# A hybrid RWKV-7 / latent-attention / mixture-of-experts layer: 128 stationary columns split in two column halves

## The chip, the cores and the metric

The kernel runs on one core of one Trainium2 chip. The metric is the device time of one launch in microseconds (us), the median of several runs. All times below are of that core. TensorE (PE in the profile) multiplies a stationary operand, loaded by LDWEIGHTS (PEld), with a moving operand that streams through the array. The array has 128 rows (the contraction, which is the partitions of both operands) and 128 columns (the stationary operand's columns, which become the output's partitions). An instruction can use a part of it: "64\*128" in a profile row is 64 rows by 128 columns. DVE is VectorE, ACT is ScalarE, POOL is GpSimd.

## The reference

The layer is computed for a prompt of 1024 tokens and a sample of 512 tokens, 1536 tokens in all, 12 tiles of 128. What bears on the change is the time mixing (a scan over tokens with a 64 x 64 state per head, 8 heads, both directions) and the router's logits:

```python
def step(state, inp):
    r_t, w_t, k_t, v_t, kk_t, a_t = inp
    sa = jnp.einsum('bhvk,bhk->bhv', state, -kk_t)
    state = (state * w_t[:, :, None, :] + sa[..., None] * (kk_t * a_t)[:, :, None, :]
             + v_t[..., None] * k_t[:, :, None, :])
    return state, jnp.einsum('bhvk,bhk->bhv', state, r_t)
...
kk = kk / jnp.maximum(jnp.sqrt(jnp.sum(kk * kk, axis=-1, keepdims=True)), 1e-12)   # per head of 64
w_log = -jax.nn.softplus(-(decay_w0[d] + jnp.tanh(wd) @ decay_up[d])) - 0.5
a = jax.nn.sigmoid(iclr_a0[d] + ad @ iclr_up[d])
...
g_prob = jax.nn.softmax((xt @ w_rg).astype(jnp.float32) + b_rg, axis=-1)   # 4 groups
e_logits = (xt @ w_re).astype(jnp.float32) + b_re                          # 32 experts
```

Around it stand adaLN modulation, an input projection of 1024 to 5120 columns, latent attention with 8 heads, a gated merge, an output projection, and a mixture of 32 experts with two experts for each token. Everything is float32.

## The kernel before

The stages run one after the other, each a block with one instruction stream for each engine, tied by semaphores: modulation and norm; input projection with the scan's operands (`project_in_and_operands`, to about 840 us); the scan (`wkv_scan`, about 840 to 1355 us); attention; the branch outputs; output projection with the router (about 1930 to 2240 us); the experts.

**Input projection and operands.** TensorE computes 40 column tiles of the projection in 20 pairs `i`. For each tile and each block of 512 tokens it runs 8 x 3 products of the split form (`split_product`, L97: L99, L100, L101). In the last 12 pairs, token tile `t = i - 8` of the scan's operands is made between those products: `gather_squares` (L551) sums the squares of k for each of 8 heads; its stationary operand `gather[:, f]` has 8 columns, and the four products (one for each 128 channels `f`, L558) accumulate in 8 partitions of `ps_8`. ACT takes the root (`root`, L631), DVE clamps and inverts (`inverse_norm`, L713), and `spread_inverse` (L561) sends the 8 values back to 128 partitions each through `spread`. `decay_and_rate` (L568) multiplies the decay and rate LoRA factors: four products each into `ps_w` and `ps_a`, contraction 64, one on the upper and one on the lower half of the rows (L580, L581), 128 stationary columns, 128 moving.

**The scan.** It works in chunks of 64 tokens, two chunks and both directions `d` for each tile `i` of 12. TensorE's order in an iteration `j` is written out by hand (L1072 to L1142). It interleaves three things: the sequential part of tile `j` (`from_state`, `from_values`, `update_state`, `update_output`, for `k` = 0 and 1); the inverse of a 64 x 64 triangular matrix for each head of tile `j + 1`, by doubling (`level_z` L986 and `level_xz` L995 for levels 1 to 4, then `half_product` L1004 and `cross_product` L1014), with transposes `turn_v`, `turn_bk` and the product `mask_v`; and `products` of tile `j + 2`. Filler products (`idle`, `dense`, `fill`) run in the first and last iterations only. The functions that the change touches:

- `products(i, d, c)` (L927, product at L939), four times an iteration: for each `f` and `g` a product with contraction 64 (row half `g`), 128 stationary columns and 128 moving columns, into PSUM tile `G`, bank `g`. After each, DVE masks `G` into `lbm` (`mask_products`, L1279) and only then the next `products` may write `G`.
- `mask_v(i, k)` (L966, product at L977), twice: 16 products with contraction 64, 128 stationary and 64 moving columns, into bank `r` of `G`. ACT copies `G` after each (`keep_mv`, L1199); the second `mask_v` waits for that. `half_product` stands between the two.
- `from_state(i, k)` (L1017, product at L1024), twice: 16 products of the same shape into `Q`, bank `g`. DVE forms `wkv_p` from it (L1314), and `from_values` needs that.

The inverse's doublings go through other engines too: after `level_z` ACT copies twice (`keep_z`, L1151, L1152) and then `level_xz` may run; after `level_xz` DVE adds and transposes (L1294, L1284) and then the next level may run.

A float32 product is carried out as two instructions, so a group of 16 products shows as x32 in the profile.

**The router.** In the output projection's stage, TensorE runs for each tile `t` two halves of the projection (24 split products each), and between them the ranks and `route` (L2559): 8 accumulating products over the model width, stationary the turned tokens `h2_t[:, k]` (128 columns), moving the router's 36 columns (L2564). DVE reads the logits (L2658) and picks groups and experts.

## Time and profile before

| what | us |
|---|---|
| median of 3 runs (lowest, highest) | 2669.66 (2669.62, 2692.78) |
| span of the profiled execution, first to last instruction | 2663.8 |
| median less that span (start and end of a launch, and the spread between executions) | 5.9 |
| TensorE busy in the span | 2463.5 |
| VectorE, ScalarE, GpSimd busy | 1564.1, 1042.1, 784.2 |

The page gives the profiled execution by its span alone; its time as a run is not shown apart from the three. In a row of the timeline the first number is the start of a group of like instructions, the second the time from there to the end of its last one; a matmul's length includes its way through the array, so consecutive groups overlap, and the distance from start to start tells how long a group holds TensorE. The last part in square brackets is idle time before the group and what ended it.

### The profile page before, as it was taken

The numbers are of one execution on the slowest core, as the hardware profiler recorded it, in microseconds if no ns is written. First come the engines' busy times: TensorE is split into PE (matmuls) and PEld (weight loads), VectorE is DVE, ScalarE is ACT, GpSimd is POOL, SyncE is SP. The second block draws the span as 40 slices with busy tenths as digits, with TensorE's granted clock in tenths as the row PEclk, the third lists the DMA queues.
The fourth block names the chain that finished last, engine by engine and source line by source line (L and its number), as shares of the span: only waits on it lengthen the run. The fifth ranks groups of instructions, "written<-read, shape, count | busy, mean of one in ns | idle before, by whom it ended". The sixth has DMA issues, their size and how long they took to land. (4 is left out here: it accounts for less than half of the span.)

```text
span 2663.8 us, 53179 instructions
## 1 busy us (share of the span) xinstructions
PE 2463.5 (92%) x22289; PEld 1932.3 (73%) x22289; DVE 1564.1 (59%) x2402; ACT 1042.1 (39%) x1855; POOL 784.2 (29%) x511
## 2 busy tenths in 40 slices
PE   5799999999997999999979889998988996999997
PEld 1488887788886999999978766666877884555554
DVE  3544458975663454554457566666886786544443
ACT  4311123343441455445445455554122221454443
POOL 0122245544442345335303300001300000444553
PEclk8899999999998999999999999999999997999998
DMA  8522224344434132332044431102755456899995
GB/s 336 204 85 79 79 97 145 128 151 147 143 136 164 55 83 71 97 94 71 19 133 111 119 91 33 31 22 104 242 166 204 160 168 237 288 360 351 357 321 113
DMA packets 196290, 399.27 MB, mean 150 GB/s; under 512 B 38698, under 2 KB 104010, under 8 KB 182994
## 3 DMA queue, kind: packets, MB, share of 16 engines
q1 hardware_dynamic: 173876, 322.58, 35.7%
q0 software_dynamic: 12960, 41.82, 5.9%
q10 hardware_dynamic: 9216, 31.46, 3.0%
q8 instruction: 178, 2.92, 0.5%
q14 instruction: 60, 0.49, 0.1%
HBM read 294.57 MB, written 106.48 MB: 151 GB/s over the span
## 5 line engine op out<-in xcount | busy, mean ns | idle before, releaser
L99 PE MATMUL ps_in<-h_t_low,w_in_high 128*128 128x512 f32 x960 | 379.4, 395 | 2.1 <-PEq L79 2.1
L100 PE MATMUL ps_in<-h_t_high,w_in_low 128*128 128x512 f32 x960 | 374.6, 390 | 0.0
L101 PE MATMUL ps_in<-h_t_high,w_in_high 128*128 128x512 f32 x960 | 374.4, 390 | 0.0
L1242 POOL TENSOR_TENSOR wkv_levels<-wkv_nt,level_mask 128x1024 f32<-128x1024 f32 x60 | 140.2, 2355 | 257.3 <-ACT wkv_nt L1191 257.3
L99 PEld LDWEIGHTS ps_in<-h_t_low,w_in_high 128*128 128x128 f32 x960 | 180.5, 188 | 44.4 <-issue 5.6
L101 PEld LDWEIGHTS ps_in<-h_t_high,w_in_high 128*128 128x128 f32 x960 | 180.6, 188 | 38.2
L100 PEld LDWEIGHTS ps_in<-h_t_high,w_in_low 128*128 128x128 f32 x960 | 180.7, 188 | 36.0
L607 ACT COPY p_row<-ps_in 128x512 f32<-128x512 f32 x72 | 42.3, 588 | 295.2 <-PE ps_in L101 258.0
L3045 PE MATMUL ps_xy<-w_tile,hidden_turned 128*128 128x512 f32 x272 | 128.4, 617 | 12.2 <-DMA w_tile<-in_w 10.9
L498 POOL CAST w_in_high<-w_in_tile 128x1024 fp32r<-128x1024 f32 x39 | 45.6, 1168 | 301.1 <-PE ps_in L101 299.0
L705 DVE TENSOR_SCALAR p_mixed<-p_row,mu_centre 128x1537 f32<-128x1537 f32 x24 | 35.3, 1471 | 149.7 <-ACT p_row L607 149.5
L2197 POOL TENSOR_TENSOR fin_y<-fin_y 128x1024 f32<-128x1024 f32 x6 | 14.5, 2414 | 365.2 <-DMA fin_y<-wkv_y 365.2
L2918 POOL DMA_INDIRECT xb<-h,row_from x34 | 47.8, 1405 | 224.6 <-DVE xb L3160 205.0
L1986 ACT ACTIVATE att_prob<-ps_scores,att_neg_max 128x1024 f32<-128x1024 f32 x64 | 71.3, 1114 | 103.7 <-DVE att_neg_max L2035 103.7
L2934 POOL TENSOR_TENSOR row_gate<-row_gate,latents_then_v 128x1024 f32<-128x1024 f32 x34 | 80.6, 2372 | 95.1 <-ACT row_gate L3121 94.9
L3045 PEld LDWEIGHTS ps_xy<-w_tile,hidden_turned 128*128 128x128 f32 x272 | 52.4, 196 | 77.1 <-issue 57.1
L500 POOL TENSOR_TENSOR w_in_low<-w_in_tile,w_in_high 128x1024 fp32r<-128x1024 f32 x39 | 106.1, 2719 | 3.1
L995 PE MATMUL ps_wkv_levels<-wkv_xt,wkv_z 64*64 64x32 f32 x3072 | 99.5, 220 | 2.8 <-issue 2.6
L986 PE MATMUL ps_wkv_levels<-wkv_x,wkv_levels 64*64 64x32 f32 x3072 | 98.9, 220 | 1.1 <-POOL wkv_levels L1242 1.1
L995 PEld LDWEIGHTS ps_wkv_levels<-wkv_xt,wkv_z 64*64 64x64 f32 x3072 | 94.0, 135 | 7.6 <-issue 4.9
L986 PEld LDWEIGHTS ps_wkv_levels<-wkv_x,wkv_levels 64*64 64x64 f32 x3072 | 93.5, 135 | 7.3 <-issue 4.0
L1931 PE MATMUL ps_prob_t<-ident,att_prob 128*128 128x128 f32 x640 | 84.1, 274 | 15.2 <-ACT att_prob_t L2000 9.6
(429 smaller groups left out, 6047.0 us busy)
## 6 DMA issues: line engine op xcount, KB each, us to landing
merged_t<-in_w SPq DMA_DIRECT2D x36, 1024.0 KB, 10.8
w_tile<-in_w SPq DMA_DIRECT2D x34, 1024.0 KB, 14.3
w_now<-in_w SPq DMA_DIRECT2D x30, 1024.0 KB, 15.0
w_ada_tile<-in_w_ada SPq DMA_DIRECT2D x12, 2048.0 KB, 9.6
wkv_in<-wkv_out SPq DMA_DIRECT2D x24, 1024.0 KB, 3.9
w_in_tile<-in_w_in SPq DMA_DIRECT2D x40, 512.0 KB, 3.6
p_t<-p_mixed ACTq DMA_DIRECT2D x24, 512.0 KB, 2.7
gates<-p_mixed ACTq DMA_DIRECT2D x16, 768.0 KB, 4.6
```

The source lines that it names most:

```text
L99: nc.tensor.matmul(out, w[0], x[1], start=start, stop=False)
L100: nc.tensor.matmul(out, w[1], x[0], start=False, stop=False)
L101: return nc.tensor.matmul(out, w[0], x[0], start=False, stop=stop)
L500: nc.gpsimd.tensor_tensor(w_lo[b][:], w[:, b], w_hi[b][:].bitcast(F32), ALU.subtract).then_inc(w_split[b], 1)
L986: mm = nc.tensor.matmul(LV[half(c), 0, h], lev[half(c), l, h], x[half(c), i % 2, h], start=True, stop=True)
L995: mm = nc.tensor.matmul(LV[half(c), 1, h], z[half(c), h], xt[half(c), i % 2, h], start=True, stop=True)
L1242: nc.gpsimd.tensor_tensor(lev[:, l], nt[:, i % 2], lmask[:, l].unsqueeze(1).to_broadcast([P, 2 * H, CH]), ALU.mult).then_inc(m["lev_ready" ...
L1931: mm = nc.tensor.transpose(ps_t[:, c, P * i:P * i + P], prob[:, n % 2, c, P * i:P * i + P], consts["ident"][:])
L1986: nc.scalar.activation(prob[:, n % 2], ps_s[n % 2][:], ACT.Exp, bias=neg_max[:, n % 2, 0:1], accum_out=total[:, n % 2, 0:1]).then_inc(m["p ...
L2918: pool.indirect_dma_start(out=xb[:, b], out_offset=None, in_=dram["h2"], in_offset=rows_at(offset), bounds_check=TOK - 1, oob_is_err=False ...
L2934: nc.gpsimd.tensor_tensor(row_gate[:, b], row_gate[:, b], gate_part[:], ALU.add).then_inc(m["row_gated"], 1)
L3045: mm = nc.tensor.matmul(ps_xy[b][:, c], hid_t[:, b, k], w2[:, b, k, 512 * c:512 * c + 512], start=(k == 0), stop=(k == F2 - 1))
```

## The change

Products with 128 stationary columns in the scan (`products`, `mask_v`, `from_state`), in its operands (`decay_and_rate`) and in the router (`route`) are written as two with 64 each, one to partitions 0 to 63 of the output and one to 64 to 127, which are the two column halves of the array. The sum of squares puts each of its four products on a strip of 32 columns: one stationary operand of 32 columns (two of them ones) serves all four, and the results lie in partitions `32 f + g`, no longer accumulated. The root, the clamp and the inverse run over 128 partitions in place of 8, the spreading operand is laid out to match, and the one memset of the inverse's tile at the start is gone.

```diff
@@ gather_squares
                 for f in range(RF):
-                    mm = nc.tensor.matmul(ps_8[0:2 * RF, 0], gather[:, f], sq[:, f], start=(f == 0), stop=(f == RF - 1))
+                    mm = nc.tensor.matmul(ps_8[32 * f:32 * f + 32, 0], gather[:], sq[:, f], start=True, stop=True)
@@ decay_and_rate
                 for f in range(RF):
-                    mw = nc.tensor.matmul(ps_w[:, f], up_w[hw, P * f:P * f + P], wa_in[hw, t % 2, 0], start=True, stop=True)
-                    ma = nc.tensor.matmul(ps_a[:, f], up_a[ha, P * f:P * f + P], wa_in[ha, t % 2, 1], start=True, stop=True)
+                    for c in range(2):
+                        out, at = slice(64 * c, 64 * c + 64), slice(P * f + 64 * c, P * f + 64 * c + 64)
+                        mw = nc.tensor.matmul(ps_w[out, f], up_w[hw, at], wa_in[hw, t % 2, 0], start=True, stop=True)
+                        ma = nc.tensor.matmul(ps_a[out, f], up_a[ha, at], wa_in[ha, t % 2, 1], start=True, stop=True)
@@ root, inverse_norm
-                nc.scalar.activation(inv8[0:2 * RF], ps_8[0:2 * RF, 0], ACT.Sqrt).then_inc(m["sqrt_ready"], 1)
+                nc.scalar.activation(inv8[:], ps_8[:, 0], ACT.Sqrt).then_inc(m["sqrt_ready"], 1)
...
-                step(nc.vector.tensor_scalar(inv8[0:2 * RF], inv8[0:2 * RF], 1e-12, None, ALU.max))
-                nc.vector.reciprocal(inv8[0:2 * RF], inv8[0:2 * RF]).then_inc(m["inv_ready"], 1)
+                step(nc.vector.tensor_scalar(inv8[:], inv8[:], 1e-12, None, ALU.max))
+                nc.vector.reciprocal(inv8[:], inv8[:]).then_inc(m["inv_ready"], 1)
...
-            step(nc.vector.memset(inv8[:], 0.0))
@@ wkv_scan
+        array_quarters = [(g, a) for g in range(2) for a in range(2)]
@@ products
-                    for g in range(2):
-                        mm = nc.tensor.matmul(G[:, g, P * f:P * f + P], bk[half(g), i % BK, d, f, pair(c)], ar[half(g), i % AR, d, f, pair(c)],
+                    for g, a in array_quarters:
+                        mm = nc.tensor.matmul(G[half(a), g, P * f:P * f + P], bk[half(g), i % BK, d, f, pair(c)][:, half(a)], ar[half(g), i % AR, d, f, pair(c)],
                                               start=True, stop=True)
@@ mask_v
-                        mm = nc.tensor.matmul(G[:, r, CH * hh(g, f):CH * hh(g, f) + CH], lbm[half(r), i % LB, 2 * d + c, hh(g, f)],
-                                              uv[half(r), i % 2, c, d, 2 * f + g], start=True, stop=True)
+                        for a in range(2):
+                            mm = nc.tensor.matmul(G[half(a), r, CH * hh(g, f):CH * hh(g, f) + CH], lbm[half(r), i % LB, 2 * d + c, hh(g, f), half(a)],
+                                                  uv[half(r), i % 2, c, d, 2 * f + g], start=True, stop=True)
@@ from_state
-                    for g in range(2):
-                        mm = nc.tensor.matmul(Q[:, g, d, CH * f:CH * f + CH], ar[half(g), i % AR, d, f, pair(c)], s0[half(g), c, f],
+                    for g, a in array_quarters:
+                        mm = nc.tensor.matmul(Q[half(a), g, d, CH * f:CH * f + CH], ar[half(g), i % AR, d, f, pair(c)][:, half(a)], s0[half(g), c, f],
                                               start=(n == 0), stop=True, skip_group_check=True)
@@ route
-                    mm = nc.tensor.matmul(ps_r[:, 0:ROUTER], h2_t[:, k], w_r[:, k], start=(k == 0), stop=(k == DF - 1))
+                    for a in range(2):
+                        at = slice(64 * a, 64 * a + 64)
+                        mm = nc.tensor.matmul(ps_r[at, 0:ROUTER], h2_t[:, k, at], w_r[:, k], start=(k == 0), stop=(k == DF - 1))
@@ operands laid out on the host
-            out["gather_heads"][CH * g:CH * g + CH, f, 2 * f + g] = 1.0
-            out["spread_heads"][2 * f + g, f, CH * g:CH * g + CH] = 1.0
+            out["gather_heads"][CH * g:CH * g + CH, g] = 1.0
+            out["spread_heads"][32 * f + g, f, CH * g:CH * g + CH] = 1.0
```

## Rows read from the trace of the kernel before

**Rows 1.** The page, part 1: busy time of each engine over the span.

```profile
PE 2463.5 (92%) x22289; PEld 1932.3 (73%) x22289; DVE 1564.1 (59%) x2402; ACT 1042.1 (39%) x1855; POOL 784.2 (29%) x511
```

**Rows 2.** Busy time by stretches: operand stage, scan, two scan iterations, one router tile.

```profile
core 0: us, PE busy (x) PEld busy (x) DVE busy (x) ACT busy (x) POOL busy (x), PEclk, DMA share, GB/s
364.00:842.00 478.00, 463.38 (x2379) 375.24 (x2377) 335.49 (x308) 183.31 (x421) 222.19 (x129) 0.99 0.40 139
840.00:1355.00 515.00, 495.86 (x12763) 468.24 (x12764) 242.57 (x459) 235.41 (x430) 207.08 (x108) 0.99 0.26 74
1013.90:1052.10 38.20, 37.77 (x1059) 36.01 (x1063) 20.26 (x40) 19.77 (x37) 17.29 (x10) 1.00 0.31 86
1052.10:1091.50 39.40, 38.20 (x1062) 36.27 (x1064) 20.25 (x40) 19.78 (x38) 17.30 (x10) 1.00 0.29 84
...
2084.60:2098.90 14.30, 14.30 (x78) 12.05 (x76) 11.80 (x36) 3.31 (x5) 0.00 (x0) 1.00 0.35 111
```

**Rows 3.** Timeline of TensorE over one scan iteration: start us, length us, engine, line.

```profile
1050.07 2.00 PE L977 MATMUL ps_wkv_g<-wkv_uv,wkv_lbm 64*128 64x64 f32 x32
1052.00 0.75 PE L1004 MATMUL ps_wkv_levels<-wkv_x,wkv_nt 32*32 32x32 f32 x64
1053.18 2.00 PE L977 MATMUL ps_wkv_g<-wkv_uv,wkv_lbm 64*128 64x64 f32 x32 [0.43 <-ACT wkv_mv L1199]
...
1056.02 2.06 PE L986 MATMUL ps_wkv_levels<-wkv_x,wkv_levels 64*64 64x32 f32 x64
1058.00 2.00 PE L1024 MATMUL ps_wkv_q<-wkv_state_decayed,wkv_alpha_rho 64*128 64x64 f32 x32
1059.93 2.05 PE L995 MATMUL ps_wkv_levels<-wkv_xt,wkv_z 64*64 64x32 f32 x64
1061.82 1.13 PE L1035 MATMUL ps_wkv_w<-wkv_p,wkv_inverse 64*64 64x64 f32 x32
...
1065.89 1.15 PE L1044 MATMUL ps_wkv_s<-wkv_uv,wkv_bk_tok 128*64 128x64 f32 x32
1066.97 1.16 PE L939 MATMUL ps_wkv_g<-wkv_alpha_rho,wkv_beta_kappa 64*128 64x128 f32 x16
...
1071.80 1.90 PE L1024 MATMUL ps_wkv_q<-wkv_state_decayed,wkv_alpha_rho 64*128 64x64 f32 x32
1073.53 1.11 PE L939 MATMUL ps_wkv_g<-wkv_alpha_rho,wkv_beta_kappa 64*128 64x128 f32 x16
...
1080.65 1.00 PE L995 MATMUL ps_wkv_levels<-wkv_xt,wkv_z 64*64 64x32 f32 x27 [0.75 <-issue]
```

**Rows 4.** Timeline of TensorE in the operand stage: gate and rate products.

```profile
380.47 0.27 PE L580 MATMUL ps_w<-prep_w_a,decay_up 64*128 64x128 f32 x1
380.48 0.27 PE L581 MATMUL ps_a<-prep_w_a,iclr_up 64*128 64x128 f32 x1
380.58 0.27 PE L580 MATMUL ps_w<-prep_w_a,decay_up 64*128 64x128 f32 x1
```

**Rows 5.** Timeline: the sum of squares in the operand stage.

```profile
373.62 1.04 PE L558 MATMUL ps_w<-cum_decay,gather_heads 128*8 128x128 f32 x8
```

**Rows 6.** Timeline: a product on four column strips in the modulation stage.

```profile
50.66 1.92 PE L218 MATMUL ps_mod<-w_ada_tile,c_silu 128*32 128x512 f32 x16
```

**Rows 7.** Timeline of the scan iteration: other engines that TensorE waits for.

```profile
1058.70 0.68 ACT L1152 ACTIVATE wkv_z<-ps_wkv_levels,block_selectors 128x512 f32<-128x512 f32 x1
...
1072.02 1.22 DVE L1279 TENSOR_TENSOR wkv_lbm<-ps_wkv_g,tri_mask 128x1024 f32<-128x1024 f32 x1 [0.16 <-PE ps_wkv_g L939]
...
1090.29 1.30 DVE L1284 STREAM_TRANSPOSE wkv_x<-wkv_xt 128x512 f32<-128x512 f32 x2
...
1091.49 1.01 ACT L1199 COPY wkv_mv<-ps_wkv_g 128x1024 f32<-128x1024 f32 x1 [2.92 <-PE ps_wkv_g L977]
```

**Rows 8.** Timeline of TensorE in the router stage: one tile's router product.

```profile
2084.66 1.95 PE L2564 MATMUL ps_router<-w_router,h_turned 128*128 128x36 f32 x16
2086.45 0.47 PE L99 MATMUL ps_out<-w_out_low,merged_high 128*128 128x512 f32 x1
```

More of the change, by code:

```diff
@@ L400, in project_in_and_operands @@
         reset = s.sb("chunk_reset", [P, RF * P])
-        gather = s.sb("gather_heads", [P, RF, 2 * RF])
+        gather = s.sb("gather_heads", [P, 32])
         spread = s.sb("spread_heads", [P, RF, P])
@@ L3422, in more_layouts @@
     out["block_selectors"] = np.stack([1 - second, second, second - 1, -second], 1)
-    out["gather_heads"] = np.zeros((P, RF, 2 * RF), np.float32)
+    out["gather_heads"] = np.zeros((P, 32), np.float32)
     out["spread_heads"] = np.zeros((P, RF, P), np.float32)
```

2 lines of the change are left out of this document (1 added, 1 removed).

## The prediction, made before the changed kernel ran

> **What bounds the kernel now.** I read the page's busy shares first: TensorE works 92% of the span and no other engine over 59% [rows 1]. Then the windows, by stage, because an average says nothing of one stage. In the scan TensorE is busy 495.9 of 515 us, in a full iteration 37.8 of 38.2 us, with DVE, ACT and POOL near 20, 20 and 17 us; in the operand stage 463 of 478 us; in a router tile 14.30 of 14.30 us, with DVE at 11.8 [rows 2]. So the three stages touched are bound by TensorE, and time taken from it counts until a wait on DVE or ACT ends last. Then the timeline of an iteration, for how long each group holds TensorE and for the distance to the waits [rows 3, 7].
>
> **What an instruction costs here.** Call a round the time in which each used part of the array does one instruction. From a group's length, less that of its last instruction (0.27 us at L580 [rows 4]; I take 0.22 for the smaller shapes and 0.6 for L218, estimates):
> - 128 stationary columns, 64 moving, two row halves: L977 and L1024 do 16 rounds, (2.00 - 0.27) / 15 = 0.115 us a round [rows 3].
> - 64 stationary columns, 64 moving: L1035 (a row half to each column half) and L1044 (all rows, two column halves), (1.14 - 0.22) / 15 = 0.06 us [rows 3].
> - 128 moving columns: L580 and L581 start 0.01 apart, the next L580 0.11 later [rows 4]. L558 loads only 8 columns and still takes (1.04 - 0.27) / 7 = 0.11 us each [rows 5]. So with 128 moving columns the moving side alone sets 0.11, and narrower stationary operands give nothing inside a round.
> - Four column strips do run at once: L218 with 512 moving columns does its 16 instructions as 4 rounds, (1.92 - 0.6) / 3 = 0.44 us [rows 6], four times the 0.11 of a fourth of the columns.
> The one thing that no row shows is two row halves and two column halves at once with 64 x 64 each. Nearest are L1044 (both column halves, all rows), L977 (both row halves, all columns), and L1004, which puts 64 instructions on four 32 x 32 parts in 0.75 us [rows 3]. At worst only two parts run at once (0.03 us an instruction, the pace of L1044); at best four (0.015). I take four, because both L1044 and L977 already fill the whole array in one round. L1004's 0.012 us an instruction says that issuing is no bound either.
>
> A change of shape costs too. L1024 holds TensorE 1.93 us between groups of other shapes, and 1.73 us where `products` of its own shape stand on both sides [rows 3]: 0.2 us for going into another shape and out. The Trainium skill says the same (TensorEngine Tiling (Array Packing), Key Properties: a change of the tiling mode drains the array). By a full drain of the 0.27 us in flight at each border the removed borders would be worth a few us more than I count; by the row, 0.2 for a pair, which I take.
>
> **Part by part, in one full iteration of the scan.** I follow TensorE's order and say by how much it is earlier, waits included. A group of `from_state` or `mask_v` becomes 64 instructions, 16 rounds of 0.06: about 1.0 us in place of 1.93.
> - `from_state`, k = 0: 0.93 less, and 0.15 for the borders, since its neighbours are 64\*64. But `level_xz` behind it waits for ACT's two copies of `level_z`, which end at 1058.70 + 0.68 = 1059.38; with 0.06 for the signal, an estimate, 1059.44, against 1059.93 now [rows 3, 7]. Gain 0.49, not 1.08.
> - `products` 0,0: 8 rounds of 0.11 stay, the border behind it goes: 0.12.
> - `products` 0,1, `from_state` k = 1, `products` 1,0: between the two `products` lies DVE's masking of the first. Now 1.73 us pass from 1071.80 to 1073.53, and the masking, which starts 0.2 later at 1072.02, ends at 1073.24, 0.29 before TensorE needs it [rows 3, 7]. With `from_state` at 0.9, DVE is late: the distance can fall to 0.2 + 1.22 + 0.06, about 1.48. Gain 0.25, with 0.1 more at each of the two borders to 64\*64: 0.45.
> - `products` 1,1: both borders go: 0.25.
> - `mask_v` k = 0: one border goes, 0.1, and 0.93 is saved; `half_product` behind it then waits for DVE's transpose, which starts at 1090.29 and needs 0.65 for its first half [rows 3, 7]. This wait is covered, for `mask_v` k = 1 has to wait for ACT's copy of 1.01 us after the first in any case. That distance (3.11 us from 1050.07 to 1053.18, of which 1.18 behind the group [rows 3]) falls by 0.8. Together 0.9.
> - `mask_v` k = 1: 0.8.
> Sum: 0.49 + 0.12 + 0.45 + 0.25 + 0.9 + 0.8 = 3.0 us, say 2.9 of 38.2. DVE, ACT and POOL keep their work, 20 us of then 35 [rows 2]. DVE's mask and ACT's `keep_z` are what comes last after the change, each once an iteration.
>
> Ten iterations have all three parts (j = 0 to 9): 29. The iteration j = 10 has no `products`: 3. The last has only the sequential chain, where both `from_state` end 0.9 earlier and DVE starts then: 1.8. Before j = 0 one pair of `mask_v` and eight `products` run among fillers: 1.8. Sum 35.6. Against it: an iteration has some 190 more pairs of load and product on 1060. The iteration with the 0.75 us stall for "issue" lasted 39.4 and not 38.2 [rows 2, 3]; I estimate 2 us more of such stalls in the scan. **Scan: -33.6 us.**
>
> **Operand stage.** The sum of squares: 8 rounds of 0.11 (L558 [rows 5]) become 2 rounds on four strips, as L218's four [rows 6]; 0.65 a tile, 12 tiles: -7.8. Its entry and exit stay: 8 columns are a strip already. `decay_and_rate`: 8 rounds of 0.11 before and after, for each of two row halves [rows 4]; 0 (its bounds stand at the third rival). The root, clamp and inverse run on 128 partitions at the same length in the free dimension, and hide behind TensorE (DVE 335, ACT 183 of 478 us [rows 2]); uncovered, nothing is added either. The dropped memset is below 1 us. **-7.8 us.**
>
> **Router.** 16 rounds with 128 stationary columns, 1.79 us from start to next start [rows 8], become 16 rounds of 0.06 on two column halves, 0.96, plus 0.2 for two new borders to the 128\*128 neighbours: -0.63 a tile. TensorE has no idle time in these tiles, DVE has 2.5 us a tile [rows 2]. Ten tiles in that rhythm, two at the end in a chain: 10 x 0.63 + 2 x 0.8 = **-8 us**. Bounds: 0 if the accumulation in one bank slows the halves, -11 if borders are free.
>
> **Sum.** -33.6 - 7.8 - 8 = -49.4 us on a span of 2663.8, so 2614.4; with the 5.9 us by which the median of the runs exceeds that span, 2620.
>
> **Rivals.**
> - *The waits take more.* TensorE's saving in `from_state` is lost wholly to `keep_z` and the masking, and half of `mask_v`'s to the copy. For it: 0.29 us of slack before the masking and a wait of 0.43 us for ACT's copy already now [rows 3, 7]. Against it: the chain of DVE and ACT was placed in the steps above with measured lengths. It gives about 1.5 us an iteration: 18 in the scan, 34 in all, 2636.
> - *TensorE starts an instruction no faster than in its 64\*64 groups.* L986 starts 64 in 1.98 us, 0.031 each [rows 3]. If that is issue and not the two halves' rounds, 64 instructions of `mask_v` and `from_state` take as long as 32 now, and only borders, squares and router gain: 22 in all, 2648. Against it stands L1004, 64 in 0.75 us, though that burst could come out of a filled queue. The Trainium skill bears on this (TensorE: Matmul & The Clock Gate, Part 1: starts never closer than about 25 ns). By that rule a group of 64 would take 1.6 us, an estimate; L1004's rows disagree with it.
> - *Only two quarters work at once, and it becomes slower.* Place: `products` and `decay_and_rate`, whose rounds of 0.11 are set by the moving side. With two quarters at a time their rounds double, since each moving operand goes in twice: +0.9 - 0.25 of border, 48 times, and +0.9, 24 times: +31 and +21. `mask_v` and `from_state` stay at 1.9: -10 by borders. Squares and router use only column parts and keep -16. Sum +26: 2696. It decides from the point where a round of quarters with 128 moving columns exceeds about 0.17 us. For it: no row shows the four. Against it: L218's four strips with four moving streams [rows 6].
> - *The change doesn't do what it says*: the halves would be ordered so that the next waits for the last. That has the effect of the previous case.
>
> **How the numbers follow.** Forecast 0.75, the waits 0.1, the pace of starts 0.09, two quarters 0.06. The forecast's own spread is 8 us to either side (stalls, borders, 0.3 us an iteration). The range reaches from 2608 to 2648 and so takes in the waits and the pace. About 1% is what a measurement of this kernel tells from no change; the line lies at 2643. Faster: the forecast, the waits, and a small part of the pace: 0.86. Same: 0.09. Slower: 0.05.
>
> **What would show it.** L1024 and L977 as x64 in about 1.1 us; L939 as x32 still near 1.1; L558 near 0.4 long; L2564 as x32 in about 1.15; idle time before L995 (ACT, 0.5) and before the third `products` (DVE, 0.6); an iteration of 35.3 us; TensorE's clock still 1.00 in the scan. It is wrong if L939 x32 takes 1.8, or if L977 x64 stays at 1.9.

## The result: slower by about 1%, and where the time went

| what | before | after |
|---|---|---|
| median of 18 runs each, on the same chips, us (lowest, highest) | 2675.12 (2662.99, 2696.94) | 2703.50 (2688.07, 2715.87) |
| ratio, 95% interval | | 1.0097 (1.0077, 1.0116) |
| span of the profiled execution | 2663.8 | 2708.2 |

The change costs about 26 us by the ratio (28 by the medians) where 49 were forecast as gain: 2703.5 lies outside the range of 2608 to 2648. The profiled execution of after is one of the longer ones (2710.0 as a run, 1.8 more than its span) and that of before one of the shorter, so the sizes below are of a difference of 44.4 us, not of 26. Here and below a run over 1.5% above the fastest of its kernel is in no ratio and in no mean clock, though it is in the medians and the lists of runs.

The record has the mean clock that TensorE was granted over each whole run. It is 0.955 on average in the 18 runs of after (0.948 to 0.961), and 0.969 in the runs of before that were made with the experiments. Within after the longer runs have the lower clock: 0.961 at 2688 and 2692 us, 0.948 at 2711. So the loss of clock described below is not a property of one profiled execution.

The page of after comes first (busy time by engine, the granted clock in 40 slices, the queue that brings instructions), then two lines of the page of before to set beside it:

```profile
PE 2460.5 (91%) x25169; PEld 1923.8 (71%) x25169; DVE 1564.8 (58%) x2401; ACT 1044.4 (39%) x1855; POOL 781.4 (29%) x511
...
PEclk9899999999997988988899989999999996999998
...
q8 instruction: 200, 3.28, 0.5%
```

```profile
PEclk8899999999998999999999999999999997999998
...
q8 instruction: 178, 2.92, 0.5%
```

TensorE is busy 2460.5 us, as before [rows 1], with 2880 more pairs of load and product (a pair is one LDWEIGHTS and one matmul). The line PEclk has five 8s between the 15th and the 20th slice (950 to 1350 us at 67.7 us a slice), where before has 9. The queue that brings instructions moved 200 packets for 178.

**Where it lies.** First starts of marked groups cut the two spans into parts (fillers L107 before the scan, the first attention product L107, first and last router product, first expert product L3050):

| from, to | before | after | difference |
|---|---|---|---|
| start, fillers before the scan | 830.5 | 822.9 | -7.6 |
| to the first product of attention | 522.2 | 573.2 | +51.0 |
| to the first router product | 718.1 | 719.5 | +1.4 |
| to the last router product | 151.0 | 148.7 | -2.3 |
| to the first expert product | 56.6 | 59.0 | +2.4 |
| to the end | 385.4 | 384.9 | -0.5 |

All of the loss is in the scan. The windows of the same 480 us of it, then those of after by stages; in the second fence the last window is a stretch with a clock of 0.53:

```profile
core 0: us, PE busy (x) PEld busy (x) DVE busy (x) ACT busy (x) POOL busy (x), PEclk, DMA share, GB/s
850.00:1330.00 480.00, 469.82 (x12418) 444.95 (x12418) 230.19 (x434) 230.25 (x422) 207.08 (x108) 1.00 0.25 71
```

```profile
850.00:1330.00 480.00, 431.79 (x13315) 407.65 (x13317) 213.05 (x397) 209.88 (x378) 193.80 (x103) 0.88 0.24 67
1036.00:1050.00 14.00, 14.00 (x252) 13.37 (x248) 4.78 (x12) 6.48 (x14) 0.00 (x0) 0.53 0.42 115
```

TensorE starts more instructions in the 480 us (13315 for 12418) and is idle five times as long (48.2 for 10.2 us), at a granted clock of 0.88 for 1.00. In after's timeline of TensorE one sees both, beside groups that went as forecast:

```profile
1068.04 1.13 PE L980 MATMUL ps_wkv_g<-wkv_uv,wkv_lbm 64*64 64x64 f32 x60
1069.74 0.75 PE L1007 MATMUL ps_wkv_levels<-wkv_x,wkv_nt 32*32 32x32 f32 x64 [0.58 <-DVE wkv_x L1287]
...
1082.91 2.06 PE L989 MATMUL ps_wkv_levels<-wkv_x,wkv_levels 64*64 64x32 f32 x64
1084.89 1.15 PE L1047 MATMUL ps_wkv_s<-wkv_uv,wkv_bk_tok 128*64 128x64 f32 x32
1085.97 1.10 PE L941 MATMUL ps_wkv_g<-wkv_alpha_rho,wkv_beta_kappa 64*64 64x128 f32 x32
...
1090.51 1.15 PE L1027 MATMUL ps_wkv_q<-wkv_state_decayed,wkv_alpha_rho 64*64 64x64 f32 x62
1092.06 1.40 PE L941 MATMUL ps_wkv_g<-wkv_alpha_rho,wkv_beta_kappa 64*64 64x128 f32 x31 [0.41 <-DVE wkv_lbm L1282]
```

These are the groups at full clock. `products` (L941) with twice the instructions takes 1.10 us as before; `from_state` (L1027) and `mask_v` (L980) take 1.15 and 1.13 for 1.90 and 2.00 [rows 3]; the third `products` waits 0.41 us for DVE's mask (0.6 forecast), `half_product` 0.58 for DVE's transpose. Now the same timeline where it went wrong:

```profile
1040.47 3.63 PE L989 MATMUL ps_wkv_levels<-wkv_x,wkv_levels 64*64 64x32 f32 x64
1044.02 1.97 PE L1047 MATMUL ps_wkv_s<-wkv_uv,wkv_bk_tok 128*64 128x64 f32 x32
1045.93 1.99 PE L941 MATMUL ps_wkv_g<-wkv_alpha_rho,wkv_beta_kappa 64*64 64x128 f32 x32
...
1072.14 0.46 PE L980 MATMUL ps_wkv_g<-wkv_uv,wkv_lbm 64*64 64x64 f32 x14 [0.69 <-issue]
...
1076.00 0.48 PE L989 MATMUL ps_wkv_levels<-wkv_x,wkv_levels 64*64 64x32 f32 x10 [1.09 <-issue]
...
1098.56 0.98 PE L941 MATMUL ps_wkv_g<-wkv_alpha_rho,wkv_beta_kappa 64*64 64x128 f32 x26 [2.04 <-issue]
```

In the first three rows every group takes nearly twice its time: L989 holds TensorE 3.55 us (1040.47 to 1044.02) for 1.98 (1082.91 to 1084.89), L1047 1.91 for 1.08, L941 1.76 for 0.94. TensorE is busy all of these 14 us: nothing is waited for, the clock of 0.53 in this window says that nearly all of it ran at the lower level of 1.2 GHz. The last three rows are waits that nothing in the profile explains ("issue"), each in or before a group of short instructions. The view of waits adds such waits up over the scan (us, times, longest), here its largest rows, after and then before:

```profile
PE ps_wkv_q L1027 <- issue: 9.0, 7, 2.2
PE ps_wkv_levels L989 <- issue: 7.6, 9, 1.4
PE ps_wkv_g L941 <- issue: 6.3, 3, 2.3
PE ps_wkv_levels L1017 <- issue: 5.2, 5, 1.6
```

```profile
PE ps_wkv_levels L995 <- issue: 2.6, 4, 0.9
...
PE ps_wkv_g L939 <- issue: 0.6, 1, 0.6
```

All "issue" rows of after together are 37 us, of before 3.2.

**Balance of an iteration.** From one `half_product` to the same one eleven iterations later, start to start: 897.2 to 1324.3 before, 897.3 to 1368.6 after, so 38.8 and 42.8 us an iteration. The three groups above ran at 1.98/3.55, 1.08/1.91 and 0.94/1.76 of their pace, about 0.55. A clock of 0.88 over 480 us is 2 x 0.12 x 480 = 115 us at half clock, of which 0.45 x 115 = 52 are lost. With 480 / 42.8 = 11.2 iterations: work (431.8 - 52) / 11.2 = 33.9, idle 48.2 / 11.2 = 4.3, half clock 52 / 11.2 = 4.6 us. Before: work 38.0, idle 0.8, half clock 0. So -4.1 + 3.5 + 4.6 = +4.0 us an iteration, +44 in eleven. The saving came, and was paid back twice: once in waits, once in clock. Of the 3.5 us of idle time 0.4 are waits for DVE and ACT (9.5 us in this window for 5.8); without issue and clock the saving is 3.7 us an iteration where the forecast, which counts these waits too, had 2.9. These sizes are estimates from windows; the rows are above.

One part of the 115 us is not the change's. At the start of the scan TensorE waits once for POOL: 2.3 us in after, at 851.5, with 20.5 us at half clock behind it. In 12 of the 13 other traces the same wait is 1.8 to 2.5 us with 10 to 20 us at half clock behind it; in that of before it is 1.1 us with none. So some 20 us of half clock, 9 us of time, separate the profiled execution of before from kernels whose scan is otherwise at full clock, which show 0.98 over this window.

### The profile page after: what moved, and what is told of

It is laid out like the page before. It is cut to its first block and busy times, and to the rows that moved or that the text cites. A ratio compares the mean times of both kernels' runs of the same rounds, so it can differ in the third digit from the quotient of the medians.

```text
span 2708.2 us, 58938 instructions
## 1 busy us (share of the span) xinstructions
PE 2460.5 (91%) x25169; PEld 1923.8 (71%) x25169; DVE 1564.8 (58%) x2401; ACT 1044.4 (39%) x1855; POOL 781.4 (29%) x511
## 3 DMA queue, kind: packets, MB, share of 16 engines
q8 instruction: 200, 3.28, 0.5%
## 5 line engine op out<-in xcount | busy, mean ns | idle before, releaser
L3050 PE MATMUL ps_xy<-w_tile,hidden_turned 128*128 128x512 f32 x272 | 123.7, 597 | 15.9 <-DMA w_tile<-in_w 14.5
L989 PE MATMUL ps_wkv_levels<-wkv_x,wkv_levels 64*64 64x32 f32 x3072 | 113.6, 232 | 9.9 <-issue 7.6
L989 PEld LDWEIGHTS ps_wkv_levels<-wkv_x,wkv_levels 64*64 64x64 f32 x3072 | 108.1, 149 | 16.8 <-issue 13.5
L998 PE MATMUL ps_wkv_levels<-wkv_xt,wkv_z 64*64 64x32 f32 x3072 | 111.7, 230 | 3.6 <-issue 2.8
L998 PEld LDWEIGHTS ps_wkv_levels<-wkv_xt,wkv_z 64*64 64x64 f32 x3072 | 107.7, 148 | 9.3 <-issue 8.2
L3050 PEld LDWEIGHTS ps_xy<-w_tile,hidden_turned 128*128 128x128 f32 x272 | 50.3, 189 | 79.2 <-issue 52.6
```

What stands on the lines that cost most here:

```text
L989: mm = nc.tensor.matmul(LV[half(c), 0, h], lev[half(c), l, h], x[half(c), i % 2, h], start=True, stop=True)
L998: mm = nc.tensor.matmul(LV[half(c), 1, h], z[half(c), h], xt[half(c), i % 2, h], start=True, stop=True)
L3050: mm = nc.tensor.matmul(ps_xy[b][:, c], hid_t[:, b, k], w2[:, b, k, 512 * c:512 * c + 512], start=(k == 0), stop=(k == F2 - 1))
```

## The experiments

The theories that I set against each other. **Supply**: TensorE takes instructions faster than they are brought, in stretches where many short ones follow; it then stands idle for "issue". **Clock**: such idle times bring the clock down, and this costs as much again. Rivals: that the quarters themselves are slow (two at a time, or a pace of starts); that the mere number of instructions does it, however slowly they are used; that the half clock comes from the way in which quarters load the array, without any idle time. The runs of one batch shared their chip and their runs of before.

### The change without its scan part

```diff
@@ changed kernel, products, mask_v, from_state as before
-                    for g, a in array_quarters:
-                        mm = nc.tensor.matmul(G[half(a), g, P * f:P * f + P], bk[half(g), i % BK, d, f, pair(c)][:, half(a)], ...
+                    for g in range(2):
+                        mm = nc.tensor.matmul(G[:, g, P * f:P * f + P], bk[half(g), i % BK, d, f, pair(c)], ...
...
```

> The changed kernel with the three scan groups (products, mask_v, from_state) as before; squares on four strips, halves in decay_and_rate and the router stay. Theory S (the loss is in the scan: TensorE's instructions come slower than the quarters use them, each stall ends in a stretch at the half clock): the stage in front of the scan 7.5 us shorter, the router 2 to 8 us shorter, the scan as before: 10 to 15 us faster than before, no issue idle above that of before. Rival Q (the halves and strips cost TensorE its clock wherever they stand): router and operands show half clock too, and the time is not below before.

Measured: 2667.08 for 2671.02 us, ratio 0.9977 (0.9944, 1.0009). The window 850 to 1330:

```profile
850.00:1330.00 480.00, 466.81 (x12209) 441.69 (x12211) 228.46 (x431) 224.55 (x412) 203.70 (x107) 0.98 0.24 68
```

PE and clock are nearly those of before, issue waits 5.2 us. So the loss is the scan's. The rest of the change gives 0.9977, 6 us less, where 10 to 15 were expected; the interval also allows no difference. The clock of 0.98 is that of most kernels here whose scan is free of long waits, below the 1.00 of the one profile of before by what stands behind the wait for POOL.

### Quarters in one function alone

Four kernels are the one before with quarters in `mask_v` only, in `products` only, in the first `mask_v` of an iteration only, and in `from_state` only.

```diff
@@ before, mask_v
-                        mm = nc.tensor.matmul(G[:, r, CH * hh(g, f):CH * hh(g, f) + CH], lbm[half(r), i % LB, 2 * d + c, hh(g, f)],
-                                              uv[half(r), i % 2, c, d, 2 * f + g], start=True, stop=True)
+                        for a in range(2):
+                            mm = nc.tensor.matmul(G[half(a), r, CH * hh(g, f):CH * hh(g, f) + CH], lbm[half(r), i % LB, 2 * d + c, hh(g, f), half(a)],
+                                                  uv[half(r), i % 2, c, d, 2 * f + g], start=True, stop=True)
@@ the same with the first mask_v alone
+                        for a in (slice(0, 64), slice(64, 128)) if k == 0 else (slice(0, 128),):
@@ before, products alone
+                    for g, a in array_quarters:
+                        mm = nc.tensor.matmul(G[half(a), g, P * f:P * f + P], bk[half(g), i % BK, d, f, pair(c)][:, half(a)], ...
@@ before, from_state alone
+                    for g, a in array_quarters:
+                        mm = nc.tensor.matmul(Q[half(a), g, d, CH * f:CH * f + CH], ar[half(g), i % AR, d, f, pair(c)][:, half(a)], ...
```

**`mask_v` alone.**

> The kernel before with mask_v alone in quarters: 64 more pairs of load and product per iteration (1060 to 1124), up to 1.7 us less TensorE work. Theory S: part of the 19 us (11 iterations) is kept, issue idle in the scan 5 to 15 us against 3, half clock in the scan 0 to 40 us: 0 to 15 us faster. Rival Q: the clock falls in the stretches of L978, issue idle as before. Rival W (waits on DVE and ACT take the gain): issue idle as before, waits on DVE and ACT up by more than 10 us, clock 1.0.

Measured: 2722.41 for 2671.02 us, ratio 1.0167 (1.0117, 1.0218). It was expected 0 to 15 us faster; it is slower than the whole change, though it saves some 2 us an iteration in TensorE's work. Its issue waits in the scan are 21 us.

**`products` alone.**

> The kernel before with products alone in quarters: also 64 more pairs per iteration, but only borders (0.4 us per iteration) to gain. Theory S: issue idle and half clock like those of e2, and with no gain to set against them 5 to 20 us slower. Rival Q: slower too, clock below 1, but issue idle as before. Rival W: 0 to 5 us faster.

Measured: 2705.22 for 2671.02, ratio 1.009 (1.0052, 1.0128), with runs from 2686 to 2727; the one with the profile is a long one, 2724.5. It was expected 5 to 20 us slower. Here rounds stay as they were, so there was next to nothing to win. Its window view, and one row of its waits from 1130 to 1190:

```profile
1090.00:1138.00 48.00, 43.43 (x1213) 41.48 (x1209) 21.48 (x40) 23.56 (x43) 17.26 (x9) 0.93 0.27 80
1138.00:1186.00 48.00, 47.89 (x794) 45.62 (x792) 12.17 (x30) 15.04 (x28) 17.23 (x9) 0.51 0.15 41
...
1278.00:1326.00 48.00, 47.89 (x789) 45.62 (x787) 13.12 (x31) 16.64 (x30) 17.23 (x9) 0.50 0.12 30
```

```profile
PE ps_wkv_levels L996 <- issue: 2.1, 1, 2.1
```

One wait of 2.1 us for issue stands at 1135.5 to 1137.6, and in the 48 us behind it TensorE is busy 47.89 us at a clock of 0.51, with 794 instructions where the window before has 1213. A group of the old form takes 1.97 us there (L1045) for 1.15. A second such stretch is the last row. This is the plainest view of the whole case: a busy share of 99% alone would hide that TensorE runs at half clock.

**The first `mask_v` alone.**

> The kernel before with only the first of the two mask_v in quarters: 32 more pairs per iteration, up to 0.9 us less work. Theory S: half of e2's stalls or less, so between before and e2 (2671 and 2722), 2665 to 2700. If the stalls were the quarters' own doing, half clock half of e2's, the same range; what it tells is from which point on the supply fails.

Measured: 2693.48 for 2670.57, ratio 1.0086 (1.0059, 1.0113). It lies in the range expected (2665 to 2700): 32 more pairs an iteration are enough for a loss.

**`from_state` alone.**

> The kernel before with from_state alone in quarters: 64 more pairs per iteration, but between groups at 0.03 us a pair, where mask_v stands next to half_product and cross_product at 0.01. Gain without stalls 0.9 us per iteration, 10 us. Theory S: fewer and shorter stalls than e2 (issue idle 5 to 15 us, half clock 20 to 80 us): 2665 to 2700. Rival Q: as much half clock as in e2, 2710 or more.

Measured: 2674.11 for 2670.57, ratio 1.0017 (0.9998, 1.0036): no difference that this tells. It saves TensorE work as `mask_v` does, and has as many pairs more; but 11 us of issue waits where `mask_v` has 21, the longest 1.9 us, and the clock is 0.97. Windows 850 to 1330 of `mask_v`, first `mask_v` and `from_state` alone, in this order:

```profile
850.00:1330.00 480.00, 451.17 (x11663) 426.28 (x11663) 209.07 (x385) 207.80 (x374) 186.76 (x97) 0.88 0.24 69
```

```profile
850.00:1330.00 480.00, 463.36 (x11527) 438.59 (x11525) 212.70 (x395) 210.98 (x378) 193.03 (x101) 0.88 0.24 69
```

```profile
850.00:1330.00 480.00, 457.62 (x12868) 430.05 (x12868) 228.33 (x430) 226.55 (x413) 204.00 (x106) 0.97 0.25 70
```

### More instructions of the old forms: quick ones and lengthy ones

No quarters here. In the first, `half_product` (32 x 32 parts, 64 instructions in 0.75 us [rows 3]) is done three times over; in the second `from_state` (64\*128, 32 instructions in 1.93 us) twice. Each writes the same values again.

```diff
@@ before, half_product
-                for h in range(H):
+                for h in list(range(H)) * 3:
@@ before, from_state
-                for n, (f, d) in enumerate((f, d) for f in range(RF) for d in range(2)):
+                for n, (f, d) in list(enumerate((f, d) for f in range(RF) for d in range(2))) * 2:
```

> The kernel before with half_product (32 x 32 parts, 64 pairs in 0.6 us) done three times over with the same result: 128 more pairs per iteration and no quarter of 64 x 64 anywhere. By its TensorE time alone 12 x 1.2 = 14 us slower. Theory S: issue idle above 10 us and half clock above 20 us in the scan, 25 to 60 us slower. Rivals Q and W: 14 us slower, issue idle and clock as before.

Measured: 2772.26 for 2671.02, ratio 1.0332 (1.0264, 1.04). Its window, and its largest waits:

```profile
850.00:1330.00 480.00, 458.79 (x11232) 435.39 (x11228) 191.80 (x356) 190.43 (x340) 174.03 (x91) 0.85 0.23 65
```

```profile
PE ps_wkv_levels L1004 <- issue: 12.5, 9, 2.6
```

128 quick pairs more, 1.4 us of work an iteration and so some 17 us in all, cost 101 us by the medians and 89 by the ratio, more than the 25 to 60 expected. Two thirds of the issue waits lie in the very function that was lengthened, nine times, 2.6 us at the longest, and the clock falls to 0.85. Neither quarters nor anything else of the change is needed for such a loss.

> The kernel before with both from_state groups done twice in their old form (128 stationary columns, 0.06 us a pair, the same result): 64 more pairs per iteration, as many as e2 and e3, but slow ones. Theory S (the pace of instructions matters, not their number): 12 x 3.6 = 43 us slower, issue idle no more than 6 us, clock 1.00 in the scan. Rival N (the number of instructions, or the program's length, matters): issue idle of 13 to 22 us and half clock of 100 us as in e2 and e3, so 80 us slower or more.

Measured: 2711.47 for 2670.57, ratio 1.0137 (1.0106, 1.0168): 41 us more by the medians, 37 by the ratio, and the work that it adds is 43 (2 x 1.9 us an iteration).

```profile
850.00:1330.00 480.00, 471.24 (x12008) 449.09 (x12009) 214.30 (x398) 210.88 (x381) 197.85 (x104) 0.98 0.24 69
```

```profile
PE ps_wkv_levels L995 <- issue: 0.8, 1, 0.8
```

64 lengthy pairs more: one issue wait in the scan, clock 0.98. As many pairs as with `mask_v` or `products` alone, which had 21 and 13 us of issue waits and clocks of 0.88 and 0.87. So it is not the number of instructions but the pace at which TensorE uses them up.

### Slowing the changed kernel down with filler products

If TensorE is only too fast for its supply, work that fills its idle time is free. `keep_busy` products of the kernel's own fillers are added to the changed kernel: at the places of `dense` in every iteration (37 us in all), or two behind `half_product` (9 us in all).

```diff
@@ changed kernel, dense
-                if j == N - 2:
-                    keep_busy(nc, consts, W[:].rearrange("p h t -> p (h t)")[:, 0:2 * RF * TOK // CH], 2)
+                if j >= 0:
+                    keep_busy(nc, consts, W[:].rearrange("p h t -> p (h t)")[:, 0:2 * RF * TOK // CH], 2 if j == N - 2 else 1)
@@ changed kernel, behind half_product (the second kernel)
                     half_product(j + 1)
+                    if 0 <= j < N - 2:
+                        keep_busy(nc, consts, W[:].rearrange("p h t -> p (h t)")[:, 0:2 * RF * TOK // CH], 2)
                     dense(j)
```

> The changed kernel with one filler product (128 x 128, 192 moving columns, result unused) at each of the seven dense places of iterations 0 to 9: 14 more pairs and some 3.7 us more TensorE work per iteration (2.3 us of products, the rest borders). By that work alone 10 x 3.7 = 37 us slower than the changed kernel, near 2740. Theory S (instructions arrive too slowly for the quarters): the fillers give the supply time, so issue idle falls under 15 us against 33 and half clock under 60 us against 130, and the kernel is no slower than the changed one, 2660 to 2700. Rivals Q (quarters lower the clock themselves) and W: 2730 to 2745.

> The changed kernel with two filler products (4 pairs, 0.65 us and borders) behind half_product alone, where the fastest groups stand, in iterations 0 to 9: 9 us of added TensorE work. Theory S: the stalls of the tail of the iteration shorten, half clock 50 to 110 us against 126: 2685 to 2705. Without an effect on supply or clock: 2712.

Measured: 2703.21 for 2670.57, ratio 1.0133 (1.0096, 1.0171), and 2689.36 for 2672.43, ratio 1.0072 (1.0042, 1.0102). With the change's 1.0097 and their own work alone they would be at 1.0235 and 1.0131. Windows 850 to 1330 of both:

```profile
850.00:1330.00 480.00, 445.98 (x13724) 406.15 (x13723) 215.51 (x401) 212.78 (x389) 200.92 (x105) 0.97 0.24 67
```

```profile
850.00:1330.00 480.00, 432.22 (x14056) 406.27 (x14054) 222.23 (x417) 221.16 (x406) 203.88 (x106) 0.96 0.24 68
```

The clock is back at 0.97 and 0.96. (The profile of the second is of its fastest run, 2672; over all runs the mean clock is 0.964 and 0.961 for the change's 0.955, so the direction holds.) In the first, issue waits fell from 37 to 28 us and not under 15, and the time is just above the 2660 to 2700 expected; in the second they stayed near 36, with the longest 3.2 us, and still the clock held better. So three quarters of the fillers' work came free in the first. In the second all of it did; that it is faster than the changed kernel, the two intervals do not tell. Neither gets back to the time of before. The second does not fit a rule by which the sum of the waits decides the clock; which waits do is open.

### Pauses of known length in the kernel before

TensorE waits, ahead of `update_state`, for small products on POOL whose only end is to make it wait: three of them in iterations 1, 3, 5 and 7, or one in each of iterations 0 to 7. TensorE gets no instruction more, save the wait. The diff is of the first; the second has `(0, 1, 2, 3, 4, 5, 6, 7), 1`.

```diff
@@ before
+        PAUSES, PAUSE_OPS = (1, 3, 5, 7), 3
...
+                if j in PAUSES:
+                    pe.wait_ge(m["paused"], PAUSE_OPS * (PAUSES.index(j) + 1))
...
+                if j in PAUSES:
+                    pool.wait_ge(m["xz_full"], 4 * (j + 1) + 3)
+                    for o in range(PAUSE_OPS):
+                        nc.gpsimd.tensor_tensor(pause_tile[:], ..., ALU.mult).then_inc(m["paused"], 1)
```

> The kernel before, in which TensorE waits in iterations 1, 3, 5 and 7 of the scan, behind the third level_xz, until GpSimd has done three small products that nothing else needs (about 2.7 us each time, an estimate). No instruction of TensorE is added. Theory S in two steps (a stall, then a stretch at the half clock): the pauses alone cost 4 x 2.7 = 11 us; each is followed by 3 to 20 us of half clock, 10 to 60 us in all, so 15 to 40 us slower. Rival (the half clock of the changed kernel comes from the shape of the groups, not from stalls): 11 us slower, clock 1.00 in the scan.

> The same with eight pauses of one such product (about 1 us each, an estimate), in iterations 0 to 7. As much pause in total. The kernel before has five stalls of up to 0.9 us in its scan and no half clock there after the first iterations; so theory S: 8 to 10 us slower, and little or no half clock. If short pauses cost the clock too: 20 us slower or more.

Measured: 2712.32 for 2672.43, ratio 1.0154 (1.0093, 1.0214), from four runs of 2696, 2697, 2727 and 2743 us, and 2684.28, ratio 1.0034 (1.0005, 1.0063). For the long pauses the waits, the timeline of TensorE behind the second one, and windows ahead of it, around it and of the whole stretch; below them waits and window of the short pauses:

```profile
PE ps_wkv_s L1046 <- POOL pause_tile L1267: 9.8, 4, 2.5
```

```profile
1062.16 1.15 PE L1046 MATMUL ps_wkv_s<-wkv_uv,wkv_bk_tok 128*64 128x64 f32 x32 [2.46 <-POOL pause_tile L1267]
...
1064.96 3.31 PE L988 MATMUL ps_wkv_levels<-wkv_x,wkv_levels 64*64 64x32 f32 x58
...
1071.09 2.05 PE L997 MATMUL ps_wkv_levels<-wkv_xt,wkv_z 64*64 64x32 f32 x64
```

```profile
1040.00:1055.00 15.00, 15.00 (x396) 14.37 (x392) 10.51 (x20) 6.59 (x16) 1.01 (x1) 1.00 0.56 145
1055.00:1070.00 15.00, 12.54 (x273) 11.72 (x270) 4.69 (x12) 6.81 (x9) 9.36 (x7) 0.78 0.15 54
850.00:1330.00 480.00, 458.48 (x11638) 433.80 (x11636) 219.55 (x405) 216.58 (x394) 212.50 (x118) 0.95 0.25 71
```

```profile
PE ps_wkv_s L1046 <- POOL pause_tile L1267: 6.9, 8, 0.9
```

```profile
850.00:1330.00 480.00, 460.99 (x11952) 436.19 (x11952) 224.44 (x418) 222.85 (x409) 209.92 (x114) 0.98 0.25 69
```

The long pauses take 9.8 us together and the short ones 6.9. With each long pause goes a stretch of half clock, of 6.8, 6.8, 3.4 and 6.8 us; the 15 us ahead of the second pause have 1.00. Behind it the first group, L1046, still takes 1.15 us, then L988 takes 3.31 us for the 1.88 of before, and nine us after the pause L997 takes 2.05 again, the length at full clock. At the first pause the clock fell 0.9 us before the pause began, behind an issue wait of 1.3 us, so that one shows nothing of the pause. The other three have no issue wait in the 7 us ahead of them. Of the eight short pauses one has half clock directly behind it (3.4 us), and one lies in a stretch that an issue wait had begun. So an idle time of some 2.5 us is followed by half clock here, one of 0.9 us mostly is not, and the quarters have no part in it.

The cost of the long pauses is uncertain, 40 us by the medians, with two runs of four 30 and 46 us longer than the others. The profiled execution is the fastest: its span of 2694.6 us is 30.8 above that of before, and 9.8 of pauses with 0.45 x 48 us of half clock (2 x 0.05 x 480) make 31. Only half of these 48 us, 24, go with the four pauses; another 20 stand behind the wait for POOL at the scan's start, which before does not have in this form. So the four pauses cost some 9.8 + 11 = 21 us in it, an estimate.

What the pauses show is also in the other traces. All 70 stretches of half clock that begin between 850 and 1340 us in the 14 traces begin in an idle wait of TensorE (of 0.35 us or more) or at most 3.1 us behind one. In after waits are so many that this alone says little; but in the scan of `products` alone there are 22, and all five of its stretches begin so. The reverse does not hold: of 37 waits of 1.8 us or more 30 are followed by half clock or lie in it, of 60 between 0.8 and 1.2 us 19, and the stretches last from 3.4 to 48 us with no order by the length of the wait.

### Squares and router alone

```diff
@@ changed kernel, back to the form before: decay_and_rate, products, mask_v, from_state
-                    for c in range(2):
-                        out, at = slice(64 * c, 64 * c + 64), slice(P * f + 64 * c, P * f + 64 * c + 64)
...
+                    mw = nc.tensor.matmul(ps_w[:, f], up_w[hw, P * f:P * f + P], wa_in[hw, t % 2, 0], start=True, stop=True)
...
```

> Only the squares on four strips and the router in two column halves; decay_and_rate and the scan as before. Squares 12 x 0.6 = 7.5 us, router 2 to 6 us: 2659 to 2663 against 2671. The scan shows no more issue idle than before.

Measured: 2667.81 for 2672.43, ratio 0.9978 (0.9952, 1.0004), five rounds; 2659 to 2663 were expected. With the first experiment's 0.9977 this is twice the same number, and both intervals take in 1. If there is a version that beats before, it is this one, by some 6 us; that is not shown.

### Eight kernels side by side

| kernel | more pairs an iteration | TensorE work at full clock per pair, ns (estimate) | issue waits in the scan, us | clock 850 to 1330 | mean clock of the runs | ratio |
|---|---|---|---|---|---|---|
| before | 0 | 36 | 3 | 1.00 | 0.969 | 1 |
| `from_state` twice, old form | 64 | 37 | 1 | 0.98 | 0.971 | 1.0137 (work 1.016) |
| first `mask_v` | 32 | 34 | 8 | 0.88 | 0.958 | 1.0086 |
| `products` | 64 | 34 | 13 | 0.87 | 0.961 | 1.0090 |
| `half_product` thrice, old form | 128 | 33 | 19 | 0.85 | 0.944 | 1.0332 (work 1.006) |
| `from_state` | 64 | 32 | 11 | 0.97 | 0.968 | 1.0017 |
| `mask_v` | 64 | 32 | 21 | 0.88 | 0.951 | 1.0167 |
| the change | 192 | 27 | 37 | 0.88 | 0.955 | 1.0097 |

The third column is 38.0 us of work an iteration and 1060 pairs, each with what the kernel adds or saves by the groups' rows (for `mask_v` alone, (38.0 - 1.9) / 1124). The fourth and fifth are of one profiled execution each, which for before is a short one of its kernel, for `from_state` alone a middle one, and for the others a long one; the sixth is over whole runs. Issue waits grow as the third column falls, from 36 ns on, but not strictly: `from_state` and `mask_v` stand at the same 32 ns with 11 and 21 us. What counts is the pace in the place: a burst of 64 instructions in 0.75 us or of quarters at 0.016 us an instruction uses up what lies ready, and the groups of 0.031 us an instruction around it must let that fill again. That is my reading of where the waits stand.

**The packets that bring TensorE's instructions.** The traces also have the time of every packet of the queue q8, and they show what the waits are for. The packets are of 16384 bytes, and there is one for each 125 or 126 of TensorE's pairs in both kernels (178 for 22289, 200 for 25169). The three issue waits of the timeline above against them, in us:

| packet sets out | lands | wait ends | from landing to the end of the wait |
|---|---|---|---|
| 1069.52 | 1070.67 | 1072.14 | 1.47 |
| 1073.56 | 1074.65 | 1076.00 | 1.35 |
| 1096.17 | 1097.05 | 1098.56 | 1.51 |

So it is with all of them: the 38 issue waits of more than 0.15 us that after has between 850 and 1330 us all end 1.2 to 1.6 us behind the landing of such a packet, and none of its 18 waits for other engines does. In the 14 traces together it is 210 of 210, and 17 of 190. Between one issue wait and the next TensorE does 127 or 128 pairs or a multiple of that, less a few: the waits stand where the instructions of one packet end. Where two follow each other directly in after, the 128 pairs take 3.3 to 5.4 us, 3.8 in the median, 0.030 us a pair, and in no scan of the 14 traces does a packet set out less than 3.2 us behind the one before it. A packet takes no longer to land in after (median 0.99 us) than in before (1.14), so it is not that the transfers became slower. This shows that the issue waits are waits for instructions. How many instructions lie ready ahead of TensorE no trace shows.

## Why the prediction was wrong, step by step

- **What bounds the stages**: right for the operand stage. In the scan no wait on DVE or ACT took the place of the saved time (9.5 us of them in the window for 5.8), but TensorE's instructions did become a bound. In the router stage DVE took back a part, see below.
- **A round costs 0.06, and four quarters work at once**: right. Group lengths of 1.13 and 1.15 us, and L941 as x32 in 1.10. In the operand stage four quarters start within 0.02 us, the next four 0.11 later:

```profile
371.80 0.43 PE L558 MATMUL ps_w<-cum_decay,gather_heads 128*32 128x128 f32 x8
372.15 0.50 PE L99 MATMUL ps_in<-h_t_low,w_in_high 128*128 128x512 f32 x1
...
377.98 0.27 PE L582 MATMUL ps_w<-prep_w_a,decay_up 64*64 64x128 f32 x1
377.99 0.27 PE L583 MATMUL ps_a<-prep_w_a,iclr_up 64*64 64x128 f32 x1
378.00 0.27 PE L582 MATMUL ps_w<-prep_w_a,decay_up 64*64 64x128 f32 x1
378.00 0.27 PE L583 MATMUL ps_a<-prep_w_a,iclr_up 64*64 64x128 f32 x1
378.09 0.27 PE L582 MATMUL ps_w<-prep_w_a,decay_up 64*64 64x128 f32 x1
```

- **Operand stage -7.8**: right, -7.6. The first row is the sum of squares, 0.35 us to the next start for 0.97 before. `decay_and_rate` takes 0.9 us as before.
- **The waits by DVE and ACT**: right in place and nearly in size for two (0.41 us ahead of the third `products` for 0.6, 0.58 ahead of `half_product`). The wait of 0.5 for ACT ahead of `level_xz` in each iteration hardly came: 0.8 us in the whole window, in two places. The rival *the waits take more* is not what happened.
- **Router -8**: the term of a tile was right: L2569 holds TensorE 1.06 us for 1.79, and in the rhythm of the middle tiles a tile takes 13.68 us for 14.30. From the first to the last router product eleven such distances should have given 6.8 us and gave 2.3, and 2.4 were lost behind them. TensorE now waits for DVE's `tile_hots` 4.8 us longer, twice as often; the cover that DVE's 2.5 us a tile gave was counted for every tile, and it did not hold for all. The wait in the whole run, after, then before:

```profile
PE ps_own_rows L2576 <- DVE tile_hots L2686: 10.1, 4, 4.5
```

```profile
PE ps_own_rows L2571 <- DVE tile_hots L2681: 5.3, 2, 4.5
```

- **"I estimate 2 us more of such stalls in the scan"**: the step that failed first. I had seen the one issue wait of 0.75 us [rows 3] and put it against the number of added pairs, 190 on 1060. Measured are 37 us for 3.2. It does not go with the number but with the pace at which a packet's instructions are used up: `from_state` twice adds 64 lengthy pairs and no wait, `half_product` thrice 128 quick ones and 16 us of waits. The prediction even held the sign in hand ("that burst could come out of a filled queue"), but only as a doubt beside the rival on the pace of starts.
- **"TensorE's clock still 1.00 in the scan"**: the step that failed next, an assumption without a price. It costs as much as the stalls or more: about 52 us in the profiled execution, some 9 of them behind the wait for POOL. By the mean clocks of all runs, 0.955 for 0.969, it is 2 x 0.014 x 2700 x 0.45 = 34 us, an estimate. The pauses show the link: an idle time of 2.5 us, and half clock behind it.
- **The sum**: scan -33.6 forecast, +51 measured. By the balance the work fell by 4.1 us an iteration (45 in eleven) and waits and clock took 8.1 (89).
- **Rivals.** *Pace of starts* fell: 62 instructions of L1027 in 1.15 us. *Two quarters at once* gave 2696, near the measured 2703.5, and is wrong all the same: L941 did not double. A time that fits is no evidence of a mechanism; the row that the prediction named for it was.

The page Runtime: NRT & Kernel Launch of the Trainium skill (Instruction fetch mechanics) says that an engine's instructions pass through a FIFO filled in blocks of 256, and that crossing a block's border is "mostly hidden". The blocks agree with this case's traces (3.28 MB in 200 packets, 16.4 KB each, one for some 126 pairs of two instructions). "Mostly hidden" holds for before, with 3.2 us of issue waits, and not for the change, with 37. Had I weighed this rule against the burst rates, the rival of a starved TensorE would have had a chance of its own.

What stays open: what makes a packet set out, and so why some issue waits are 0.7 us and others over 2; why `from_state` alone is nearly spared, with as many pairs as `mask_v`, though it stands between slower groups; which waits bring half clock, and what ends it.

## What to carry to other kernels

Splitting instructions to fill the array pays in TensorE's time and costs in instructions: look first at how many ns of work there are for each pair of load and product, around the place and not only on average, and at whether "issue" shows up at all; here an average of 36 ns was already the edge, and the packets of 128 pairs never set out less than 3.2 us apart in the scan (0.025 us a pair). Read TensorE's clock beside its busy share in every stage, since half clock looks like full work. Where an edit makes TensorE faster than its supply, a filler can cost nothing beside the gap that it fills, but the kernel without the gap was faster still.

## What the runs showed of the hardware that I had not expected

- TensorE fully busy does not mean that it is soon at full clock: 47.89 of 48 us busy at 0.51, twice in one scan. The Trainium skill (TensorE: Matmul & The Clock Gate, Part 1) has the lower clock as that of an idle or cold array and the full one as that of a busy one; by these rows the array stayed at the lower one while it was busy, and the pace of its groups (1.97 us for 1.15) bears the clock out.
- At the lower clock the groups shown, loads included, take 1.8 times their time at the full one (3.55 us for 1.98, 1.91 for 1.08), not twice.
- TensorE's instructions come in packets of 16384 bytes, 127 or 128 pairs of load and product in the scan, and an issue wait ends 1.2 to 1.6 us behind the landing of one (210 of 210).
- Four 64 x 64 parts with float32 operands run at once, with starts 0.00 to 0.01 us apart, and 128 moving columns need 0.11 us a round with two parts at work (L580, L581 before) as with four.
- A wait of 2.5 us, made with no change to TensorE's work, went with a fall of the clock three times of four, and at the fourth the clock was down already; one of 0.9 us did so once in eight.
